# ScalarE's order in the first stage: shift row, small weight and decay column

## What is computed

```
ada = silu(c) @ w_ada + b_ada                 # c: 1 x 1024, w_ada: 1024 x 3072
shift, scale, gate = split(ada, 3)
h    = rmsnorm(x, norm_w) * (1 + scale) + shift
proj = h @ w_in                               # z, xbc, dt_raw, q, k, v, z_att, f_logit, g_logit
...
dt = softplus(dt_raw + dt_bias)
a  = dt * (-exp(a_log))                       # 16 heads: the decay column
```

## Time and profile before

| | us |
|---|---|
| median of 3 runs | 2006.11 |
| lowest and highest | 2005.21, 2006.27 |
| the profiled execution, device time | 2004.76 |
| its span, first to last instruction | 2003.1 |
| TensorE busy | 1894.8 |
| VectorE busy | 1166.8 |
| ScalarE busy | 786.0 |

### The profile page before, as it was taken

How to read it: one execution, slowest core, us unless ns; L and a number is a source line. 1 busy time by engine, 2 the same in 40 slices (tenths; PEclk the granted TensorE clock), 3 DMA queues, 4 the chain that set the end, 5 groups by cost and what they waited for, 6 DMA issues and landing times. The chain is left out here.

```text
span 2003.1 us, 26401 instructions
## 1 busy us (share of the span) xinstructions
PE 1894.8 (95%) x9508; PEld 1530.0 (76%) x9508; DVE 1166.8 (58%) x1492; ACT 786.0 (39%) x1198; POOL 163.3 (8%) x319
## 2 busy tenths in 40 slices
PE   6899999999999999999999999789999998999997
PEld 3678787878787887888888888567777777887776
DVE  5576445455456777767777444488333335664865
ACT  4422442434324435444544332252244444442322
POOL 1000100100100000000000100012100001110100
PEclk9899999999999999999999999999999999999999
DMA  8541555644431121222114733423301111211202
GB/s 275 200 76 43 85 108 103 104 128 137 147 105 53 53 54 51 65 74 73 53 53 159 250 105 116 136 54 89 113 25 42 34 31 43 64 43 54 99 30 95
DMA packets 169153, 181.20 MB, mean 90 GB/s; under 512 B 10994, under 2 KB 143530, under 8 KB 168298
## 3 DMA queue, kind: packets, MB, share of 16 engines
q1 hardware_dynamic: 155024, 130.69, 20.6%
q0 software_dynamic: 13760, 49.30, 11.2%
q10 hardware_dynamic: 282, 0.09, 0.0%
HBM read 139.56 MB, written 40.50 MB: 90 GB/s over the span
## 5 line engine op out<-in xcount | busy, mean ns | idle before, releaser
L298 PE MATMUL acc<-ha_hi,w_hi 128*128 128x512 f32 x640 | 258.9, 405 | 5.6 <-ACT stash L311 4.4
L298 PE MATMUL acc<-ha_hi,w_lo 128*128 128x512 f32 x640 | 250.7, 392 | 0.0
L298 PE MATMUL acc<-ha_lo,w_hi 128*128 128x512 f32 x640 | 250.4, 391 | 0.0
L281 PE MATMUL acc<-ha_hi,w_hi 128*128 128x512 f32 x592 | 189.6, 402 | 29.3 <-DVE ha_lo L2170 13.6
L281 PE MATMUL acc<-ha_lo,w_hi 128*128 128x512 f32 x592 | 185.9, 396 | 0.0
L281 PE MATMUL acc<-ha_hi,w_lo 128*128 128x512 f32 x592 | 185.4, 395 | 0.0
L265 DVE TENSOR_TENSOR w_lo<-w_raw,w_hi 128x1024 fp32r<-128x1024 f32 x96 | 117.5, 1224 | 76.2 <-ACT w_hi L261 72.8
L281 PEld LDWEIGHTS acc<-ha_hi,w_hi 128*128 128x128 f32 x592 | 111.4, 192 | 60.7 <-issue 16.4
L298 PEld LDWEIGHTS acc<-ha_hi,w_hi 128*128 128x128 f32 x640 | 120.8, 189 | 30.8 <-issue 6.5
L298 PEld LDWEIGHTS acc<-ha_hi,w_lo 128*128 128x128 f32 x640 | 120.7, 189 | 26.5
L298 PEld LDWEIGHTS acc<-ha_lo,w_hi 128*128 128x128 f32 x640 | 121.0, 189 | 22.7
(11 more groups left out here) (489 smaller groups left out, 3680.0 us busy)
## 6 DMA issues: line engine op xcount, KB each, us to landing
w_raw<-in_w_in SPq DMA_DIRECT2D x99, 512.0 KB, 4.1
acs_bc<-acs_scr POOLq DMA_DIRECT2D x8, 1024.0 KB, 16.0
w_raw<-in_w_out SPq DMA_DIRECT2D x11, 512.0 KB, 3.8
x_tok<-in_x SPq DMA_DIRECT2D x8, 512.0 KB, 7.0
w_scale<-in_w_ada SPq DMA_DIRECT2D x8, 512.0 KB, 9.7
w_shift<-in_w_ada SPq DMA_DIRECT2D x8, 512.0 KB, 9.0
xt_scr<-xt SPq DMA_DIRECT2D x1, 4096.0 KB, 17.7
w_ada_g<-in_w_ada SPq DMA_DIRECT2D x8, 512.0 KB, 10.1
```

The source lines that it names most:

```text
L281: mm = pe.matmul(acc[:, n % 2, h * HALF:(h + 1) * HALF], w[:, n % 2, k, :], x[:, k, h * HALF:(h + 1) * HALF], start=(k == 0 and i == 0), s ...
L298: mm = pe.matmul(acc[:, 0, half * HALF:(half + 1) * HALF], w[:, n % 2, k, :], x[:, k, half * HALF:(half + 1) * HALF], start=(k == 0 and i ...
```

## The change

Only the order of instructions in act_0 changes; no instruction is added or taken away. The diff:

```
-            for i in range(EARLY_RAW, NT):
+            for i in range(EARLY_RAW, NT - 1):
                 for g in range(2):
                     copy_xt(i, g)
-            act.wait_ge(col_loaded, 16 * 8)
-            act.activation(neg_a[:, :], neg_a[:, :], ACT.Exp)
-            act.drain()
-            act.activation(neg_a[:, :], neg_a[:, :], ACT.Copy, scale=-1.0)
             act.wait_ge(w_part, 16)
             split_hi(act, N_SMALL1)
             act.wait_ge(shift_added, KT)
             for h in range(2):
                 at = SHIFT_AT[h]
                 act.activation(shift_row[0:1, h * HALF:(h + 1) * HALF], work[at, h, :], ACT.Copy).then_inc(silu_c_done, 1)
+            for g in range(2):
+                copy_xt(NT - 1, g)
             act.wait_ge(dve_steps, 2)
             for f in range(KT):
...
             split_hi(act, N_XBC)
+            act.wait_ge(col_loaded, 16 * 8)
+            act.activation(neg_a[:, :], neg_a[:, :], ACT.Exp)
+            act.drain()
+            act.activation(neg_a[:, :], neg_a[:, :], ACT.Copy, scale=-1.0)
             end_stage(act, 0)
```

## The result

| | before | after |
|---|---|---|
| median of the runs compared | 2006.01 (5 runs, 2004.21 to 2006.27) | 1991.95 (5 runs, 1987.57 to 1996.64) |
| ratio | | 0.9928, 95% interval 0.9914 to 0.9942 |
| profiled execution, device time | 2004.76 | 1991.95 |
| its span | 2003.1 | 1990.4 |

The change takes 14.1 us off the median (the interval: 12 to 17). Forecast were 12.0, with a range of 1991.7 to 1997.5. The median lies just inside it at its fast end; by the ratio, applied to the 2006.11 the forecast stood on, the time is 1991.67, just outside. So the direction and the mechanism held and the size was taken too small. In a second comparison the same kernel gave 0.9935 (0.9923 to 0.9948), which lies inside the range. All 12 executions of it in this case have a median of 1991.97, all 63 of the kernel before one of 2005.21: 13.2 us.

A forecast was written before the change was run, and what follows sets the result against it. Bound: the shift row waiting in ScalarE's queue behind the column transfers while TensorE idles. Gains of 10.47 (L635's start) and 1.5 (its clock) make 12.0 us less, median 2006.11 to 1994.1; range 1991.7 to 1997.5.

The forecast's parts named there:

- The bound: First stage: TensorE idles 10.47 us before L635 because ScalarE's shift row copy queues behind the wait for the column transfers.
- Gain 10.47 from the start of L635: First stage: with the shift row copied right behind its matmuls, L635 starts at 44.45 instead of 54.92.
- Gain 1.5 from L635's clock: L635's sixteen small matmuls take 2.05 us instead of 3.57 at nearly full clock; bounds 0 and 1.6.
- The choice between them: Clock at L635: taken to return at the same place, half under the transposes, full from 44.65; forecast's chance 0.66.
- rival 3: No clock fall before the transposes in most executions: L635 from 43.1 to 45.05, 13.4 us less, 1992.7; chance 0.08.
- The range: 1991.7 to 1997.5: lowest run less 13.5, to highest less 10.5 with a tail of 1.0 and cold slice of 0.7.
- Small weight: ScalarE, first stage: its split moved ahead runs from 38.2 to 39.3 in idle time and costs nothing.
- Projection, tail: First stage: cold first projection costs 0, two and a half cold slices hidden; TensorE covers ScalarE's final exponential with 0.4 spare.
- Rival 2: ScalarE's tail sets the first stage's end because of a drain before the table load: 1 us given back, 1995.1; chance 0.05.
- Transfers: Store of xt lands at 62.8, 2 us before the conv_in pads; earlier w_raw and w_ada_g loads cost nothing.
- Rival 4: Next stage gives part of the gain back through store, w_raw and w_ada_g loads standing closer together: about 1999; chance 0.04.
- The transposes and the clock: First stage: clock rose at 44.65 behind transposes, against the skill's rule; by that rule the gain is 10.5, not 12.0.

The follow-up runs named there:

- column_only: Kernel before with only the exponential of neg_a moved to the stage's end; split and shift row stay behind the xt copies: median 1996.08, ratio 0.9956.
- column_between: Changed kernel with neg_a's exponential and sign change, and the columns' wait, put between the last xt copy and the first ha_hi slice: median 1999.28, ratio 0.9974.
- before_again: Kernel before, run again without any edit: ratio 1.0008, eleven executions between 2004.60 and 2009.28.
- split_late: Changed kernel with the small weight's split put back behind the shift row and the last xt copies: median 1994.59, ratio 0.9941.
- columns_early: Kernel before with one GpSimd wait removed, so the eight column transfers are issued from 3 us on; ScalarE's order unchanged: median 2005.50, ratio 1.0004.
- shift_first: Changed kernel with the last raw transposes behind the sixth shift pair, the last pair before the sums, last xt copies before the split: median 1990.41, ratio 0.9927.
- after_again: Changed kernel, run again without any edit on a second chip job, five executions: median 1991.99, ratio 0.9935.

## Where the prediction was right, and where it was wrong

*The bound.* Right. The row stood behind the columns' wait; column_only and column_between each take off one side of it (8.8 and 5.2 us), and with L637 directly behind the transposes the gap is 0 as forecast.

*Gain 10.47 from the start of L635.* This term was mis-sized. It was right for a trace with half clock under the last transposes; with full clock there, the start moves from 54.92 to 43.18, 11.74. Of the 1.27 more, 0.95 is the transposes (1.97 and 1.02 from their start to where L635's matmuls begin or could begin) and 0.58 the last shift matmuls (1.54 and 0.96 to the start of the transposes), less 0.27 by which the sums started later in that execution (39.33 for 39.06). In the kernel before it does not matter which clock the transposes meet (before_again), so the rows of before could not price it by a difference in time.

*Gain 1.5 from L635's clock.* Right in size where the clock was full: 1.94 in three profiles of four, a gain of 1.63. It was 3.57 in the fourth, a gain of 0, and 2.21 where the clock fell halfway, in column_only.

*The choice between them.* This is the step that failed: "I take it that the clock comes back in the same place". One execution showed half clock under the transposes, and it was made the likeliest for all. The runs put in its place: full clock throughout in three of four profiles of the changed kernel (13.4 to 13.5 less), half throughout in one (9.9). My rival 3, with 13.4 less and 1992.7, was priced right to 0.1 us and was the commonest case, but had a chance of 0.08. The mean of the four, 12.5, and the 13.2 of all executions together are not far from the forecast, but that is luck: it is a mean of cases of which none is the forecast's own. What turns the clock at one moment or the other in the same program stays open.

*The range.* Its fast end was the lowest of three runs less 13.5, 1991.7. It had room for the first stage alone. From the second stage to the end the profiles of this case take 1917.4 to 1922.8 us with the same program there, and the kernel before spreads from 2002.5 to 2009.3 over 63 executions. Three runs within 1.1 us hid that. By the ratio the measured time is 0.03 us outside, with an interval of 1988.9 to 1994.5, so on which side of the bound it fell is chance; that the bound stood so near the commonest case is the mistake.

*Small weight.* Right: the split ran at 38.40, with no wait. That the move was also worth 1.5 us through VectorE's order (split_late) was not said: the working named only the time on ScalarE.

*Projection, tail.* Right: the first has at least 2.4 us of cover. In the second ScalarE's last operation ended at 63.30 and TensorE's at 63.68, 0.4 as forecast. Rival 2 did not happen.

*Transfers.* The order of landing held, the times did not, and the cover was smaller than said. The store took 19.8 us instead of 17.7, and landed at 64.4; the pads of conv_in, cleared at 64.49, were released by it:

```profile
64.49 0.11 POOL L889 MEMSET conv_in<- 128x6 f32 x1 [21.31 <-DMA xt_scr<-xt]
```

w_raw of the next stage, issued at 45.1, landed 20.9 later at 66.0, 1.6 after the store as before, and 2.1 us later than the stage wanted it. Most of the store's length goes with the broadcast in front of it: it took 12.1 in columns_early, where the columns had long landed, 13.2 in shift_first, where it was issued ahead of the broadcast, and 17.7 to 19.8 in all the others. The last 1 to 2 us are open. The loads issued right behind it do not explain them alone, since column_between has them too and took 18.5, near the 18.3 of before_again. Nothing was lost, because TensorE needs that weight a projection later, at 75.65; this second cover, which the forecast named, held. Rival 4 did not happen.

*The transposes and the clock.* Before, the clock had come back at 44.65 behind shift matmuls and transposes. In after_again it stayed at half through the same work and was full again only in the projection (0.94 in the slice 57.5 to 58.0). The rule of the Trainium skill ("TensorE: Matmul & The Clock Gate", Part 4: PE-mode transpose) that transposes don't count as work is neither shown nor refuted by this: no run has transposes alone.

## What to carry to other kernels

On an engine that takes its instructions in order, look for a wait whose result nobody needs yet and count what stands behind it on that engine: here a column first read in the next stage held the row that everything waited for. Take the wait away at its place in the order rather than at its source, unless you know what the earlier transfer pushes aside. And when a change puts a short stretch of TensorE work on the chain that a wait had covered, price it at both clocks and give each case its chance: one profile shows one of them.

## What the runs showed of the hardware that I had not expected

- The same program meets half clock at different moments: the eight last transposes took 1.09 or 1.97 us and the sixteen one-column matmuls 1.94 or 3.57, which made 3.5 us in one stage.
- Eight small column transfers, among them two of d_skip with 2 KB each, issued at the start delayed the last pair of shift matmuls by 9.6 us. Issued 2.3 us behind a 4 MB store and beside the loads after it, d_skip landed 19.8 us after issue instead of 10.7. The 4 MB store itself took 12.1 us with no column transfer under way, and 17.7 to 19.8 behind them.
- A tensor_scalar of 128x1024 on GpSimd (1.7 us) stretched the tensor_tensor on VectorE beside it from 1.23 to 1.90 us, and left a tensor_scalar at 0.81.
